# Seventh product behind the sixth and third in every Strassen group, and the decay rows spread in two parts

## The chip, the cores and the metric

The kernel runs on one core of one Trainium2 chip. The metric is the device time of one execution in microseconds. The kernel before was timed three times: 1894.62 us in the median, 1892.29 at the lowest and 1895.87 at the highest.

## The reference

Two blocks of a language model follow one another on 256 tokens of 2048 features, all in fp32. What matters here are the matrix products of the second block and the weights that they read:

```
merged = sigmoid(g_a) * (y_a @ w_up_a) + sigmoid(g_b) * (y_b @ w_up_b)   # g_a, g_b: columns of h @ w_in
x = x + merged @ w_o
hid = rmsnorm(x) @ w_ffn_in            # 2048 x (2 * 5632)
x = x + (silu(hid[:, :5632]) * hid[:, 5632:]) @ w_ffn_out
x = x + sigmoid(rmsnorm(x) @ w_ple_gate) * (p @ w_ple)
```

The first block has two recurrent layers ahead of its output product, an mLSTM with decay factors for each token and head, and an HGRN2 whose output h_b of 1024 features is normalised per head. Both lie beside the products of the first block's weights.

## The kernel before

**Pieces.** Every weight matrix is cut into pieces of two 128-row chunks by 512 columns (two such chunks, 512 KB in all). Piece g goes through four stations in a ring of four buffers (RING = 4). SyncE loads it into `raw`. ScalarE writes the high part of its fp32 values (`whi`, line 928, or line 1177 in a Strassen group), once TensorE has finished piece g-4. VectorE writes the rest (`wlo`, line 1876, or `s_lo`, line 2556). TensorE multiplies the high and low part of the activations by `whi` and the high part by `wlo`: twelve products of 128x512 for a standard piece (lines 1359 and 1364), six for a Strassen piece (lines 1724 and 1728). Every engine runs through the pieces in one written order, and whatever else an engine does is put between two pieces by a test on g or on (slab, piece).

**Strassen groups.** Twelve groups c = 0 to 11 compute two slabs of output columns by Strassen's seven products: groups 0 to 2 give the gates of the merge (`w_in`), groups 3 to 11 gates of the feed-forward part (`w_ffn_in`). A product M1 to M7 has four quarters q along the 2048 rows, so a group has 28 pieces in `S_ORDER`. `add_block` weaves them with standard pieces of other matrices: in most groups ten, one ahead of about every four Strassen pieces; the last group has 16. The products take their weights from different places:

- M1 from b11, loaded into the four quarters of `r1`; M5 from a sum that lies in the DRAM tensor `summed`, loaded into `r1` once M1's pieces are split (`load_fifth`, 1 MB twice).
- M2 from b21, M7 from another sum in `summed` ("seventh"): halves of 512 KB (`load_half`, line 788). M6's addend and M3's weights are both b22, also a half. All halves share the four slots raw[4..7]. `plan_s_loads` hands the slots out in the order of first use; a load waits until the piece that read its slot last has been split (`lo_ready`).
- M6 from r1 + b22, added by VectorE two Strassen pieces ahead (`s_sum`, line 2551, `S_LEAD` = 2).
- M4 from r1 + b21, added in place by an accumulating DMA of GpSimd (line 898), issued when M6.q has been split.

SyncE issues all its loads in one sorted order and waits at each until its place is free. `s_copies` (ScalarE) copies the sums of M1, M5 and M6 out of PSUM, `s_gates` (VectorE, three operations) forms the outputs after the last of M3 and M7, `s_silu` or sigmoids follow. M6 adds onto the sums of M1 and M3 onto those of M5, each once they have been copied; M7 has a PSUM bank of its own. `u_product` (VectorE) multiplies a product of `w_up_a` or `w_up_b` by its gate.

**Ahead of the groups.** `ml_cols` (TensorE) stands after piece (10, 7) of the first block: four transposes of 4x4, then eight products of 4x256 that spread rows of decay factors over 128 partitions into two PSUM buffers ("bc", 0) and ("bc", 1). VectorE reads them in slab 11. The scaling of hB, one half at a time (w counts VectorE's steps, L0 is 23 or 49), stands at step L0 + 30, line 2251; `hg_qd` and `hg_kd` (lines 2018 to 2027) are operands of TensorE's line 1431.

Of the kernel before, what the change touches and what calls it, by code (L numbers as in the profile page):

```python
# [39 lines left out]
S = 256  # L40
# [71 lines left out]
S_GROUPS = len(BLOCKS)  # L112
S_ORDER = [(m, q) for m in ("M1", "M2", "M7", "M5") for q in range(4)] \
    + [("M6", 0), ("M6", 1), ("M3", 0), ("M6", 2), ("M3", 1), ("M6", 3), ("M3", 2), ("M3", 3)] + [("M4", q) for q in range(4)]
S_LEAD = 2
# [199 lines left out]
def two_blocks_kernel(nc, A, out):  # L315
# [4 lines left out]
    with ctx:  # L320
# [338 lines left out]
        def _(sp):  # L659
# [130 lines left out]
            for free, need, kind, to, what in PLAN.loads:  # L790
                copies_for_sums(need)
                if kind == "pair":
                    load_ffn(free, need, to, what)
                if kind == "r1":
                    load_r1(free, to, what)
                if kind == "fifth":
                    load_fifth(free, to, what)
                if kind == "half":
                    load_half(free, to, *what)
                if kind == "resid":  # L800
                    sp.wait_ge(lo_ready, free + 1)
                    sp.wait_ge(piece_used, S_AT[M_GROUPS - 1, "M3", 3] + 1)
                    sp.wait_ge(sem("resid_held"), 16)
                    sp.dma_start(resid[:, :, to * COLS:(to + 1) * COLS], held[:, :, to * COLS:(to + 1) * COLS])\
                        .then_inc(sem(f"resid_back{to}"), 16)
                if kind == "p":
                    u_used(sp, "uB", 2)
                    sp.wait_ge(sem("p_held"), 32)
                    for x in range(2):
                        sp.dma_start(pT[1][x].bitcast(F32).rearrange("p k s -> p (k s)"), held_p[:, x]).then_inc(sem("p_back"), 16)  # L810
# [95 lines left out]
        def _(act):  # L906
# [272 lines left out]
            def s_copies(g, c):  # L1179

                if g == S_AT[c, "M2", 3]:
                    s_done(act, c, "M1")
                    if 0 < c < M_GROUPS and MERGE_S[c] == 2:
                        u_used(act, "uA", 0)
                    act.activation(hid_of(c)[:, 0, :], s_bank(c, "M1"), ACT.Copy).then_inc(sem("s_first"), 1)
                if g == S_AT[c, "M5", 3] + 3:
                    s_done(act, c, "M5")
                    if 0 < c < M_GROUPS:
                        u_used(act, "uB", max(0, MERGE_S[c] - 2))
                    act.activation(second_of(c)[:, 1, :], aux[:, 1, :], ACT.Copy).then_inc(sem("s_fifth"), 1)  # L1190
                if g == S_AT[c, "M6", 3] + 3:
                    act.wait_ge(piece_used, S_AT[c, "M6", 3] + 1)
                    act.activation(second_of(c)[:, 0, :], s_bank(c, "M6"), ACT.Copy).then_inc(sem("s_sixth"), 1)
# [6 lines left out]
            for kind, g, *x in PLAN.merge:  # L1200
# [22 lines left out]
                for c in range(M_GROUPS):  # L1223
                    s_copies(g, c)
                    if g == S_AT[c, "M3", 3] + 7:
                        act.wait_ge(sem("s_gate_in"), c + 1)
# [39 lines left out]
            for kind, g, *x in PLAN.ffn:  # L1266
# [22 lines left out]
                for c in range(M_GROUPS, S_GROUPS):  # L1289
                    s_copies(g, c)  # L1290
                    if g == S_AT[c, "M3", 3] + 7:
                        s_silu(c)


            for t, (g, n, role, _, q, p) in enumerate(PLAN.tail):
                split_hi(g)
                if g == S_AT[S_GROUPS - 1, "M3", 3] + 7:
                    s_silu(S_GROUPS - 1)
# [23 lines left out]
        def _(pe):  # L1322
# [161 lines left out]
            def ml_cols():  # L1484
# [7 lines left out]
                ins.then_inc(aux_full, 1)  # L1492
                for i in range(2):
                    u = AUX[("bc", i)]
                    free(u)
                    for h in range(2):
                        ins = pe.matmul(bank(u)[:, h * S:(h + 1) * S], sel[:, 2 * i + h, :], hrow[:, 3, :], start=True, stop=True)
                    ins.then_inc(aux_full, 1)

# [23 lines left out]
            for s in range(16):  # L1523
                n = FIRST["A"] + s
                for p in range(8):
# [25 lines left out]
                    if (s, p) == (10, 7):  # L1551
                        ml_cols()
                    if (s, p) == (11, 4):
                        ml_scores()
# [129 lines left out]
            def s_piece(g, c, m, q):  # L1684
# [12 lines left out]
                if m == "M2" and q == 0 and c > 0:  # L1697
                    pe.wait_ge(sem("hid_odd_ready"), c)
                    pe.wait_ge(sem("tr_taken"), fills_before(g, "a"))
                if m == "M7" and q == 0:  # L1700
                    pe.wait_ge(sem("merge_forms_lo" if c < M_GROUPS else "forms_lo"), 4)
# [162 lines left out]
        def _(dve):  # L1864
# [335 lines left out]
            for s in range(16):  # L2200
                for p in range(8):
# [22 lines left out]
                    for half, L0 in enumerate(HG_START):  # L2224
# [20 lines left out]
                        if w == L0 + 27:  # L2245
                            dve.wait_ge(sem("ss_hB"), half + 1)
                            variance(f"hB{half}", HG_E)
                        if w == L0 + 30:
                            powered(dve, f"hB{half}")
# [316 lines left out]
            def s_gates(c):  # L2566

                s_done(dve, c, "M3")
                dve.wait_ge(sem("s_sixth"), c + 1)
# [33 lines left out]
            for kind, g, *x in PLAN.merge:  # L2603
# [25 lines left out]
                for j in range(4):  # L2629
                    for role in ("uA", "uB"):  # L2630
                        if g == slab_end(role, j) + (2 if slab_end(role, j) in PLAN.block_end else 3):
                            u_product(role, j)
                for c in range(M_GROUPS):
                    if g == S_AT[c, "M2", 3] + 3:
                        s_up(c)
                    if g == S_AT[c, "M3", 3] + 3:
                        s_gates(c)
# [82 lines left out]
            def between(g):  # L2720
# [12 lines left out]
                for c in range(M_GROUPS, S_GROUPS):  # L2733
                    if g == S_AT[c, "M2", 3] + 3:
                        s_up(c)
                    if g == S_AT[c, "M3", 3] + 3:
                        s_gates(c)
# [113 lines left out]
```

## Time and profile before

| | |
|---|---|
| median of three runs | 1894.62 us |
| lowest, highest | 1892.29, 1895.87 us |
| profiled execution | 1893.05 us |
| its span | 1891.3 us |
| granted clock of TensorE, mean | 0.999 |

The page has for each engine its busy time and its share of the span:

| engine | busy us | share |
|---|---|---|
| TensorE, products | 1877.2 | 99% |
| TensorE, weight loads | 1641.9 | 87% |
| VectorE | 1471.8 | 78% |
| ScalarE | 1140.8 | 60% |
| GpSimd | 130.4 | 7% |
| DMA queue of SyncE, share of 16 engines | | 63.3% |
| DMA queue of GpSimd, share of 16 engines | | 20.6% |

A row of a timeline says when an instruction (or a run of equal ones) began, how long it ran, its line, what it wrote and read, and in brackets how long its engine had been idle before it and what released it. `ple<-...` in the groups is `r1`, which shares its memory. The chain of work that ended last consists of TensorE for 90%, VectorE for 5% and DMA for 3% of the span.

### The profile page before, as it was taken

How to read it: one execution, taken by the hardware profiler on the slowest of the kernel's cores; microseconds unless marked ns; L12 is line 12 of the kernel's file. 1: busy time of each engine (PE TensorE's matmuls, PEld its weight loads, DVE VectorE, ACT ScalarE, POOL GpSimd, SP SyncE). 2: the span in 40 equal slices, each digit the busy share in tenths (PEclk: the TensorE clock that was granted, in tenths of full speed). 3: DMA queues.
4: the chain of work that ended last, by engine and by line, in shares of the span. 5: the costliest groups of instructions: out<-in, count | busy, mean ns of one | idle time of the engine just before them, and what ended most of it. 6: DMA issues, size and time to landing. Idle time of an engine off the chain costs nothing.

```text
span 1891.3 us, 23371 instructions
## 1 busy us (share of the span) xinstructions
PE 1877.2 (99%) x9018; PEld 1641.9 (87%) x9018; DVE 1471.8 (78%) x1591; ACT 1140.8 (60%) x1417; POOL 130.4 (7%) x156
## 2 busy tenths in 40 slices
PE   9999999999999999999999999999999999999998
PEld 8888888888888888888888888888888888888887
DVE  6889776655666677778888657988998999898865
ACT  7556445555566556566766455666766676666553
POOL 4000011000001100000000000000000000000000
PEclk9999999999999999999999999999999999999999
DMA  9799898999989879998797886788878887987653
GB/s 392 267 284 310 274 309 272 330 347 327 309 290 312 271 269 299 321 315 278 295 313 247 330 256 239 254 311 284 276 254 320 280 271 257 327 260 249 219 188 130
DMA packets 86815, 535.95 MB, mean 283 GB/s; under 512 B 10416, under 2 KB 11184, under 8 KB 40752
## 3 DMA queue, kind: packets, MB, share of 16 engines
q1 hardware_dynamic: 72736, 458.69, 63.3%
q0 software_dynamic: 13824, 75.50, 20.6%
q8 instruction: 72, 1.18, 0.2%
q10 hardware_dynamic: 144, 0.26, 0.0%
q14 instruction: 39, 0.32, 0.0%
HBM read 529.69 MB, written 105.38 MB: 336 GB/s over the span
## 4 chain that ended last, share of the span: by engine, by line
PE 90%; DVE 5%; DMA 3%; issue 1%; ACT 1%; POOL 0%; SPq 0%; ACTq 0%; DVEq 0%; POOLq 0%
PE acc L1359 44%; PE acc L1364 22%; PE aux L1724 12%; PE aux L1728 6%; DVE wlo L2556 2%; PE aux L1338 2%; DMA ple<-in_w_ffn_in 1%; DVE wlo L1876 1%; PE aux L1431 1%; DVE ple L2551 1%; DMA ple<-in_w_in 1%; DMA raw<-summed 1%; PE aux L1805 0%; ACT whi L928 0%; ACT whi L1177 0%
## 5 line engine op out<-in xcount | busy, mean ns | idle before, releaser
L1876 DVE TENSOR_TENSOR wlo<-raw,whi 128x1024 fp32r<-128x1024 f32 x512 | 623.8, 1226 | 296.4 <-ACT whi L928 288.4
L928 ACT ACTIVATE whi<-raw 128x1024 fp32r<-128x1024 f32 x511 | 534.0, 1054 | 449.8 <-PE acc L1364 414.1
L1359 PE MATMUL acc<-whi,actA_hi 128*128 128x512 f32 x892 | 344.0, 386 | 0.7 <-ACT whi L928 0.7
L1359 PE MATMUL acc<-whi,actA_lo 128*128 128x512 f32 x892 | 339.1, 380 | 0.0
L1359 PE MATMUL acc<-whi,actB_hi 128*128 128x512 f32 x796 | 304.5, 383 | 0.2 <-DVE actB_lo L2673 0.2
L1359 PE MATMUL acc<-whi,actB_lo 128*128 128x512 f32 x796 | 301.7, 379 | 0.0
L1177 ACT ACTIVATE whi<-ple 128x1024 fp32r<-128x1024 f32 x192 | 201.0, 1055 | 139.4 <-PE acc L1364 55.6
L2556 DVE TENSOR_TENSOR wlo<-ple,whi 128x1024 fp32r<-128x1024 f32 x192 | 230.2, 1220 | 31.3 <-ACT whi L1177 28.5
L1364 PE MATMUL acc<-wlo,actA_hi 128*128 128x512 f32 x892 | 229.1, 379 | 0.0
L1364 PE MATMUL acc<-wlo,actB_hi 128*128 128x512 f32 x796 | 204.4, 379 | 0.0
L2556 DVE TENSOR_TENSOR wlo<-raw,whi 128x1024 fp32r<-128x1024 f32 x144 | 174.2, 1220 | 30.6 <-ACT whi L1177 28.9
L1359 PEld LDWEIGHTS acc<-whi,actA_hi 128*128 128x128 f32 x892 | 169.1, 190 | 25.5 <-issue 2.0
L1177 ACT ACTIVATE whi<-raw 128x1024 fp32r<-128x1024 f32 x144 | 152.0, 1055 | 64.3 <-PE acc L1364 36.5
L1364 PEld LDWEIGHTS acc<-wlo,actA_hi 128*128 128x128 f32 x892 | 168.9, 189 | 24.2
L1359 PEld LDWEIGHTS acc<-whi,actA_lo 128*128 128x128 f32 x892 | 169.2, 190 | 23.4 <-issue 0.5
L1359 PEld LDWEIGHTS acc<-whi,actB_hi 128*128 128x128 f32 x796 | 150.5, 189 | 21.6 <-DVE actB_lo L2673 1.0
L1364 PEld LDWEIGHTS acc<-wlo,actB_hi 128*128 128x128 f32 x796 | 150.4, 189 | 21.6 <-DVE wlo L1876 0.3
L1359 PEld LDWEIGHTS acc<-whi,actB_lo 128*128 128x128 f32 x796 | 150.6, 189 | 20.6
L1724 PE MATMUL aux<-whi,actB_hi 128*128 128x512 f32 x360 | 136.8, 380 | 0.8 <-ACT whi L1177 0.8
L1724 PE MATMUL aux<-whi,actB_lo 128*128 128x512 f32 x360 | 136.4, 379 | 0.0
L1728 PE MATMUL aux<-wlo,actB_hi 128*128 128x512 f32 x360 | 107.4, 380 | 0.9 <-DVE wlo L2556 0.8
L1724 PE MATMUL aux<-whi,actA_hi 128*128 128x512 f32 x216 | 83.0, 384 | 0.0
(366 smaller groups left out, 2377.0 us busy)
## 6 DMA issues: line engine op xcount, KB each, us to landing
raw<-in_w_in SPq DMA_DIRECT2D x108, 1024.0 KB, 7.3
raw<-in_w_ffn_out SPq DMA_DIRECT2D x44, 1024.0 KB, 6.9
summed<-in_w_ffn_in POOLq DMA_DIRECT2D x36, 1024.0 KB, 11.6
raw<-in_w_ffn_in SPq DMA_DIRECT2D x72, 512.0 KB, 7.9
ple<-summed SPq DMA_DIRECT2D x24, 1024.0 KB, 4.9
raw<-summed SPq DMA_DIRECT2D x48, 512.0 KB, 5.4
ple<-in_w_ffn_in SPq DMA_DIRECT2D x18, 1024.0 KB, 6.9
ple<-in_w_ffn_in POOLq DMA_DIRECT2D x36, 512.0 KB, 9.9
```

Of the source, the lines that this page charges most:

```text
L928: act.activation(whi[:, g % RING], raw_piece(g), ACT.Copy).then_inc(hi_ready, 1)
L1177: act.activation(whi[:, g % RING], s_source(c, m, q), ACT.Copy).then_inc(hi_ready, 1)
L1338: ins = pe.transpose(bank(u)[:, c * S + t * P:c * S + (t + 1) * P], src[:, t, (c0 + c) * P:(c0 + c + 1) * P], ident[:, :])
L1359: pe.matmul(acc2(n)[:, t, :], act[x][:, k + c, t * P:(t + 1) * P], woven(whi, g, c), start=(p == 0 and c == 0 and x == 0), stop=False)
L1364: ins = pe.matmul(acc2(n)[:, t, :], act[0][:, k + c, t * P:(t + 1) * P], woven(wlo, g, c), start=False, stop=(last and c == PK - 1))
L1431: ins = pe.matmul(bank(u)[:, c], Kp[n % 2][:, c], Qp[n % 2][:, c], start=True, stop=True)
L1724: pe.matmul(o, lhs(x, q * PK + k), woven(whi, g, k), start=(q == 0 and k == 0 and x == 0 and not onto), stop=False, skip_group_check=onto)
L1728: ins = pe.matmul(o, lhs(0, q * PK + k), woven(wlo, g, k), start=False, stop=(q == 3 and k == PK - 1), skip_group_check=onto)
L1876: dve.tensor_tensor(wlo[:, g % RING], raw_piece(g), whi[:, g % RING].bitcast(F32), ALU.subtract)\
L2551: dve.tensor_tensor(x, x, half_slot(c, S_ADDEND[m], q), ALU.add).then_inc(sem("s_sum"), 1)
L2556: dve.tensor_tensor(wlo[:, g % RING], s_source(c, m, q), whi[:, g % RING].bitcast(F32), ALU.subtract)\
```

## The change

In every group M7 moves from behind M2 to behind M6 and M3, and M6 and M3 take turns strictly: M1, M2, M5, then M6.0, M3.0, M6.1, M3.1, M6.2, M3.2, M6.3, M3.3, then M7, M4. What hung on the last piece of M3 (`s_gates`, `s_silu`, a load of `resid`) hangs on the last of M7; a wait for the summed activations moves from M7 to M5, the copy of M5 comes one piece earlier, and `u_product("uB", 2)` two pieces later. In the first block the eight spreading products are cut into four after piece (10, 7) and four after (11, 0), and the scaling of hB stands one step later.

```diff
-S_ORDER = [(m, q) for m in ("M1", "M2", "M7", "M5") for q in range(4)] \
-    + [("M6", 0), ("M6", 1), ("M3", 0), ("M6", 2), ("M3", 1), ("M6", 3), ("M3", 2), ("M3", 3)] + [("M4", q) for q in range(4)]
+S_ORDER = [(m, q) for m in ("M1", "M2", "M5") for q in range(4)] \
+    + [(m, q) for q in range(4) for m in ("M6", "M3")] + [(m, q) for m in ("M7", "M4") for q in range(4)]
...
-                    sp.wait_ge(piece_used, S_AT[M_GROUPS - 1, "M3", 3] + 1)
+                    sp.wait_ge(piece_used, S_AT[M_GROUPS - 1, "M7", 3] + 1)
...
-                if g == S_AT[c, "M5", 3] + 3:
+                if g == S_AT[c, "M5", 3] + 2:
...
-                    if g == S_AT[c, "M3", 3] + 7:
+                    if g == S_AT[c, "M7", 3] + 7:
...
-                for i in range(2):
-                    u = AUX[("bc", i)]
-                    free(u)
-                    for h in range(2):
-                        ins = pe.matmul(bank(u)[:, h * S:(h + 1) * S], sel[:, 2 * i + h, :], hrow[:, 3, :], start=True, stop=True)
-                    ins.then_inc(aux_full, 1)
+
+            def ml_rows_spread(i):
+                u = AUX[("bc", i)]
+                free(u)
+                for h in range(2):
+                    ins = pe.matmul(bank(u)[:, h * S:(h + 1) * S], sel[:, 2 * i + h, :], hrow[:, 3, :], start=True, stop=True)
+                ins.then_inc(aux_full, 1)
...
                         ml_cols()
+                        ml_rows_spread(0)
+                    if (s, p) == (11, 0):
+                        ml_rows_spread(1)
...
-                if m == "M7" and q == 0:
+                if m == "M5" and q == 0:
                     pe.wait_ge(sem("merge_forms_lo" if c < M_GROUPS else "forms_lo"), 4)
...
-                        if w == L0 + 30:
+                        if w == L0 + 31:
...
-                s_done(dve, c, "M3")
+                s_done(dve, c, "M7")
...
-                        if g == slab_end(role, j) + (2 if slab_end(role, j) in PLAN.block_end else 3):
+                        last = slab_end(role, j)
+                        if g == last + (2 if last in PLAN.block_end else 5 if (role, j) == ("uB", 2) else 3):
...
-                    if g == S_AT[c, "M3", 3] + 3:
+                    if g == S_AT[c, "M7", 3] + 3:
                         s_gates(c)
```

## Rows read from the trace of the kernel before

**Rows 1.** The page's head and its first part.

```profile
span 1891.3 us, 23371 instructions
...
PE 1877.2 (99%) x9018; PEld 1641.9 (87%) x9018; DVE 1471.8 (78%) x1591; ACT 1140.8 (60%) x1417; POOL 130.4 (7%) x156
```

**Rows 2.** Waits of the weight load, 840 to 1800 us: us in total, times, longest us.

```profile
PEld aux L1728 <- DVE wlo L2556: 4.7, 8, 1.2
PEld aux L1724 <- ACT whi L1177: 1.8, 3, 1.2
```

**Rows 3.** Timeline of TensorE around 1028: start us, us, line, xcount [idle before <-releaser].

```profile
1025.47 0.38 PE L1724 MATMUL aux<-whi,actB_hi 128*128 128x512 f32 x1
...
1026.76 0.38 PE L1724 MATMUL aux<-whi,actB_hi 128*128 128x512 f32 x1
...
1028.58 0.70 PE L1728 MATMUL aux<-wlo,actB_hi 128*128 128x512 f32 x2 [0.79 <-DVE wlo L2556]
1029.12 0.38 PE L1359 MATMUL acc<-whi,actA_hi 128*128 128x512 f32 x1
```

**Rows 4.** Timeline of ScalarE at 863 and at 1025.

```profile
863.26 1.06 ACT L1177 ACTIVATE whi<-raw 128x1024 fp32r<-128x1024 f32 x1 [4.64 <-DMA raw<-summed]
...
1025.02 1.06 ACT L1177 ACTIVATE whi<-ple 128x1024 fp32r<-128x1024 f32 x1 [3.41 <-DMA ple<-in_w_in]
```

**Rows 5.** Timeline of TensorE, 273.8 to 280.5.

```profile
274.14 1.97 PE L1497 MATMUL aux<-hrow,sel 4*128 4x256 f32 x8
276.04 0.51 PE L1359 MATMUL acc<-whi,actA_hi 128*128 128x512 f32 x1
...
280.42 0.38 PE L1359 MATMUL acc<-whi,actA_hi 128*128 128x512 f32 x1
```

**Rows 6.** Stretches: from:to length, busy (xcount) per engine, PEclk, DMA share, GB/s.

```profile
276.30:279.80 3.50, 3.50 (x10) 2.72 (x10) 3.46 (x11) 0.00 (x0) 0.00 (x0) 0.51 1.04 274
218.00:219.70 1.70, 0.00 (x0) 0.00 (x0) 1.66 (x4) 0.00 (x0) 0.00 (x0) 1.00 1.05 188
```

**Rows 7.** Timeline of VectorE, 156 to 162.

```profile
158.79 1.22 DVE L2251 TENSOR_TENSOR hg_v<-hg_v,rstd 128x1024 f32<-128x1024 f32 x1
```

**Rows 8.** Timeline of TensorE, 160 to 162.7.

```profile
161.46 1.16 PE L1431 MATMUL aux<-hg_qd,hg_kd 128*128 128x128 f32 x8 [0.75 <-DVE hg_kd L2027]
```

**Rows 9.** Timeline of ScalarE, 1206 to 1212.

```profile
1206.90 1.06 ACT L1177 ACTIVATE whi<-ple 128x1024 fp32r<-128x1024 f32 x1 [0.24 <-PE aux L1728]
```

**Rows 10.** Timeline of VectorE, 1204 to 1212.

```profile
1206.70 3.82 DVE L2556 TENSOR_TENSOR wlo<-ple,whi 128x1024 fp32r<-128x1024 f32 x3
1210.43 1.22 DVE L2551 TENSOR_TENSOR ple<-ple,raw 128x1024 f32<-128x1024 f32 x1
```

**Rows 11.** Timeline of GpSimd's DMA issues, 1279 to 1300.

```profile
1280.96 0.86 POOL L898 DMA_DIRECT2D ple<-in_w_ffn_in  x1 [54.12 <-DVE wlo L2556]
1282.09 0.86 POOL L898 DMA_DIRECT2D ple<-in_w_ffn_in  x1 [0.27 <-DVE wlo L2556]
1287.05 0.86 POOL L898 DMA_DIRECT2D ple<-in_w_ffn_in  x1 [4.10 <-DVE wlo L2556]
1291.59 0.86 POOL L898 DMA_DIRECT2D ple<-in_w_ffn_in  x1 [3.68 <-DVE wlo L2556]
```

**Rows 12.** Timeline of SyncE's DMA issues, 1276 to 1300.

```profile
1279.56 0.33 SPq L763 DMA_DIRECT2D raw<-in_w_ffn_out  x1
1284.10 9.83 SPq L788 DMA_DIRECT2D raw<-in_w_ffn_in  x4
```

**Rows 13.** DMA, 1280 to 1300: queues, then issues (KB each, median us to landing).

```profile
q0 software_dynamic: 576, 2.10, 56.2%
q1 hardware_dynamic: 653, 2.94, 40.6%
...
ple<-in_w_ffn_in POOLq DMA_DIRECT2D x4, 512.0 KB, 8.9
raw<-in_w_ffn_in SPq DMA_DIRECT2D x4, 512.0 KB, 8.5
```

**Rows 14.** DMA, 1343 to 1360: issues.

```profile
raw<-in_w_ffn_in SPq DMA_DIRECT2D x4, 512.0 KB, 9.8
```

**Rows 15.** The page's sixth part: DMA issues.

```profile
raw<-summed SPq DMA_DIRECT2D x48, 512.0 KB, 5.4
```

**Rows 16.** Groups of instructions by line, VectorE.

```profile
L2718 DVE TENSOR_TENSOR resid<-resid,acc 128x1024 f32<-128x1024 f32 x20 | 24.3, 1213 | 0.4 <-PE acc L1364 0.4
```

More of the change, by code:

```diff
@@ L1290, in _ @@
                     s_copies(g, c)
-                    if g == S_AT[c, "M3", 3] + 7:
+                    if g == S_AT[c, "M7", 3] + 7:
                         s_silu(c)
@@ L1296, in _ @@
                 split_hi(g)
-                if g == S_AT[S_GROUPS - 1, "M3", 3] + 7:
+                if g == S_AT[S_GROUPS - 1, "M7", 3] + 7:
                     s_silu(S_GROUPS - 1)
@@ L2735, in between @@
                         s_up(c)
-                    if g == S_AT[c, "M3", 3] + 3:
+                    if g == S_AT[c, "M7", 3] + 3:
                         s_gates(c)
```

## Prediction, made before the change was run

> **What bounds the kernel now.** I read the page's head first: TensorE is busy 1877.2 of 1891.3 us [rows 1], and its mean granted clock is 0.999 of full speed, so the time is the number of its columns plus its gaps. The profiled run took 1893.05 us with 1.75 us outside its span; the median of the three timed runs, 1894.62 us, is 1.57 us more, and I add that at the end. The change adds and removes no product of any size. It can therefore only close gaps, open gaps, or change the clock. The next views are the waits ahead of TensorE over the Strassen groups [rows 2], one gap of each kind in the timelines [rows 3 to 8], and then what the new order leans on: how far ScalarE and VectorE run ahead [rows 9, 10] and what the DMA queues do while M6 and M3 run [rows 11 to 15].
>
> Six products of a Strassen piece take 1.29 us from start to start (1025.47 to 1026.76) [rows 3], so a standard piece of twelve takes 2.59. I count time from the start of M5.0 in the new order. The places are M5.0 to M5.3 at 0, 1.3, 2.6, 3.9; a standard piece at 5.2; M6.0 7.8, M3.0 9.1, M6.1 10.4, M3.1 11.7; standard 13.0; M6.2 15.5, M3.2 16.8, M6.3 18.1, M3.3 19.4; standard 20.7; M7.0 to M7.3 at 23.3, 24.6, 25.9, 27.2; standard 28.5; M4.0 at 31.1.
>
> **What it takes away.**
> (a) The waits for M4. M4's weights are r1 plus b21, added by a POOL DMA that starts when M6.q is split. In the group at 1028 M4.3 starts 1.29 after M4.2, but its last products wait for the low half of its weights, and the next piece starts at 1029.12: 2.36 for a piece of 1.29, a gap of 1.06 [rows 3]. ScalarE began that split at 1025.02 after 3.41 us of waiting for the DMA [rows 4]; at VectorE it then stood in the queue. Over the groups the eight waits for the low half add up to 4.7 us [rows 2]. M6.3 moves four pieces towards the front (three Strassen, one standard: 3 x 1.29 + 2.59 = 6.5 us), more than 3.41, so these waits go. u_product(uB,2) moves behind one more piece and has no consumer near: nothing.
> (b) M7's weights in the first group come by loads that end too late: ScalarE waits at 863.26 for 4.64 us [rows 4], TensorE 1.8 us in three waits [rows 2]. M5 takes that place; its two loads are issued as soon as M1's pairs of quarters are split, ahead of M7's in the same queue, and a wait of TensorE for them shows nowhere. So these go. (a) and (b) are 6.5 us by the waits; each wait also costs some 0.1 to 0.2 of restart that the row doesn't count, so I take 7.0.
> (c) The spread of the decay rows. Eight four-row products take 1.97 us [rows 5]; right behind them the granted clock is 0.51 of full speed, its 1.2 GHz level, for 3.5 us [rows 6], and the piece from 276.04 to 280.42 takes 4.38 instead of 2.59 [rows 5]: 1.8 us. With four of them behind (10,7) and four behind (11,0), 1 us each, a full piece stands between. An idle engine over 1.7 us left the clock at 1.00 [rows 6], so a lone 1 us of small products ought not to lower it. I take 1.8 us as gained; the other bound is nothing gained. The second part is read by vector work three pieces later: no wait.
> (d) The scaling of the first half of hB, 1.22 us of VectorE at 158.79 [rows 7], stands ahead of the products of the gate that TensorE waits for 0.75 us at 161.46 [rows 8]. One step later it stands behind them, and the gap shrinks from 0.75 plus restart to nothing: 1.0 us. For the second half there is no such wait on the page: nothing.
> Together 7.0 + 1.8 + 1.0 = 9.8 us.
>
> **What it adds: a wait for M7's weights.** M7's four halves ("seventh", 512 KB each, from `summed`) share four slots with b21 and b22, given out in order of first use. In the old order M7 came before M6 and took the slots that M2 had freed. Now M7 comes after M3, and each of its loads waits until M3.q has been split. So when is M3.q split? ScalarE starts the split of piece g 0.24 us after TensorE has left piece g-4 and takes 1.06 [rows 9]; VectorE takes 1.22 for the low half, 3.82 for three, and 1.22 more for each sum of M6.q [rows 10]. Through nine splits and four sums VectorE is the later of the two. Stepping through the places gives the ends of the M3 splits at 8.2, 11.6, 16.2 and 18.4. Counting back from the products that read the low half (0.86 into a piece), a split must start 1.44 us ahead of its piece: at 21.9, 23.2, 24.4 and 25.7 for M7.0 to M7.3. The four loads thus have 13.7, 11.6, 8.2 and 7.3 us.
>
> How long do they take? In the old order the same moment had the same traffic, with b21 of the next group in M7's place: four adds from 1280.96 to 1291.59 [rows 11], a 1 MB load at 1279.56 and four halves from 1284.10 [rows 12]. There the halves took 8.5 us in the median, the adds 8.9 [rows 13]; in another group 9.8 [rows 14]. Alone, a load from `summed` takes 5.4 [rows 15], but the adds are now all under way beside M7's loads (issued 5.4 to 17.6). By single loads M7.3 lands at 18.4 + 8.5 = 26.9 or 18.4 + 9.8 = 28.2, against 25.7: 1.2 or 2.5 us late. By volume: the software queue took 56.2% of 20 us for 2.10 MB, four adds, so 2.8 us of all sixteen engines each; the hardware queue 40.6% for 2.94 MB, so 1.45 for a half and 2.9 for 1 MB [rows 13]. Four adds, four halves and the 1 MB load are 19.9 us. From the first issue at 5.4, with some 2.5 us in which little moves (the start of the first transfer, and the thin start of the queue), all is landed at 27.8: 2.1 late. I take 2.0 us of stall for M7.3, with 1.2 and 2.5 as ends. M7.2 (16.2 + 8.5 = 24.7 against 24.4) stalls by part of it only.
>
> The groups 0 to 10 are alike; the last one has 16 standard pieces between, over 10 us from M3.3 to M7.3, and no stall. 11 x 2.0 = 22 us. After such a stall VectorE has no lead, and in three groups an addition to the residual (1.21 us) [rows 16] falls on M4: 0.8 each, 2.4 us. Elsewhere the extra vector operations keep at least 0.5 us of slack. The gates, their activations and the load of `resid` hang on M7.3 now instead of M3.3; each is the last piece ahead of M4 and the standard piece before it, so nothing there moves. M5's copy on ScalarE comes a piece earlier and finds 2 us of slack; the loads of M5 and of M6's addends are issued no later than before and are needed 15 us on: nothing.
>
> **Sum.** 22 + 2.4 - 9.8 = +14.6 us: 1893.05 + 14.6 = 1907.7, and with the 1.57 of the median 1909.2. I forecast 1909.
>
> The Trainium skill speaks against this price. Its page "DMA: Bandwidth & Descriptors", section "Anatomy of one DMA — SWDGE (gpsimd) path", gives about 2 us plus the bytes over 436 GB/s; an estimate by it is 3.2 us for 512 KB, below the 7.3 allowed, and the sum would be -9.8. The 8.5 to 9.8 us of these rows disagree wherever adds run beside the load. The same page's "Arbitration" says that a DMA engine turns between its queues packet by packet, which agrees with those rows.
>
> **Rivals.**
> (B) M7's loads are in time. If they take 7.3 us or less, no stall: 1893.05 - 9.8 = 1883.3, median 1884.8. For it: the 5.4 us of a load alone [rows 15], and the M3 splits are spread over 10 us, so that the adds are thinner than at 1280. Against it: all groups' medians that I read lie at 8.5 or above in that stretch, and the volume leaves no room.
> (C) A small stall. At 0.9 us per group, 10 us, the gains are used up: 1894.6. It wants halves of 8.2 us.
> (D) Heavier. With 9.8 us for each, M7.2 is 1.6 late and M7.3 2.5; 11 x 2.5 = 27.5, + 3.5 behind it, - 9.8 = +21: 1916. If such a gap lowers the clock for 3.5 us as at 276, 1.8 us more in each hit group; for half of them +10: 1926.
> (E) The split of the small products doesn't hold the clock up: +1.8 on any case. A part of each range, not a case of its own.
>
> **How the numbers follow.** A difference within 0.2% (3.8 us) can't be told from none. Forecast (stalls of 1.2 to 2.5; 1899 to 1916): 0.66. D: 0.13. C, which ends within 0.2%: 0.11. B, faster: 0.10. Of the forecast's lowest part little falls under 1898.4, so slower is 0.78, same 0.12, faster 0.10. The range leaves out B and the end of D: 1892 to 1924.
>
> **What would show it.** In the changed kernel: ScalarE's L1177 waiting for `raw<-summed` ahead of M7.3, and TensorE gaps of some 2 us at L1724 or L1728 in M7 eleven times; the seventh halves at 8 to 10 us instead of 5.4; no gap at M4.3; M5 at 864 without one; the granted clock at 1.00 from 276 to 280; no wait at L1431 near 161. Wrong it is if the halves issued behind the M3 splits take under 7.3 us, or if those splits end well before 18.4.

## The result, and the profile after

The changed kernel takes 1936.64 us in the median of four runs (1931.02 to 1938.94), against 1893.68 for the kernel before (median of four, 1892.29 to 1895.87): a ratio of 1.022, 95% interval 1.0202 to 1.0239. The forecast was 1909, with a range up to 1924. The direction was right and the size was not: +43 us instead of +14.6.

The page of the changed kernel, its head, its first part, one group of the fifth and three of the sixth (issues: KB each, median us to landing):

```profile
span 1935.5 us, 23369 instructions
...
PE 1892.7 (98%) x9018; PEld 1649.4 (85%) x9018; DVE 1471.0 (76%) x1591; ACT 1138.9 (59%) x1417; POOL 130.7 (7%) x156
...
L1177 ACT ACTIVATE whi<-raw 128x1024 fp32r<-128x1024 f32 x144 | 151.7, 1054 | 108.3 <-DMA raw<-summed 78.0
...
raw<-in_w_ffn_in SPq DMA_DIRECT2D x72, 512.0 KB, 5.0
...
raw<-summed SPq DMA_DIRECT2D x48, 512.0 KB, 8.2
...
ple<-in_w_ffn_in POOLq DMA_DIRECT2D x36, 512.0 KB, 9.0
```

No engine has more to do than before; TensorE's share fell from 99% to 98% and its busy time rose from 1877.2 [rows 1] to 1892.7, which is the sign of a lower clock, since the products are the same 9018: the mean granted clock fell from 0.999 to 0.992. The halves from `summed` take 8.2 us in the median instead of 5.4 [rows 15], and ScalarE spends 78.0 us waiting for them.

The waits of the weight load from 840 to 1900 us, which answer to [rows 2]:

```profile
PEld aux L1728 <- ACT whi L1177: 35.6, 14, 4.1
PEld aux L1732 <- DVE wlo L2560: 6.7, 11, 1.0
```

Before, these two rows were 1.8 us in three waits and 4.7 in eight. Now the high part of a piece is waited for in 14 places, 35.6 us.

One group of the eleven begins with M5.0 at 1279.64. SyncE's issues in the timeline of the changed kernel, which answer to [rows 12]:

```profile
1287.85 3.73 SPq L788 DMA_DIRECT2D raw<-summed  x2
1292.39 0.33 SPq L763 DMA_DIRECT2D raw<-in_w_ffn_out  x1
1295.80 4.23 SPq L788 DMA_DIRECT2D raw<-summed  x2
```

GpSimd's issues in the same timeline, which answer to [rows 11]:

```profile
1285.14 0.86 POOL L898 DMA_DIRECT2D ple<-in_w_ffn_in  x1 [55.12 <-DVE wlo L2560]
1289.25 0.86 POOL L898 DMA_DIRECT2D ple<-in_w_ffn_in  x1 [3.25 <-DVE wlo L2560]
1293.79 0.86 POOL L898 DMA_DIRECT2D ple<-in_w_ffn_in  x1 [3.68 <-DVE wlo L2560]
1297.29 0.86 POOL L898 DMA_DIRECT2D ple<-in_w_ffn_in  x1 [2.63 <-DVE wlo L2560]
```

ScalarE at M7.2 and M7.3 in that timeline:

```profile
1307.08 1.06 ACT L1177 ACTIVATE whi<-raw 128x1024 fp32r<-128x1024 f32 x1 [6.27 <-DMA raw<-summed]
1308.36 1.06 ACT L1177 ACTIVATE whi<-raw 128x1024 fp32r<-128x1024 f32 x1 [0.22 <-DMA raw<-summed]
```

TensorE from M7.1's last products to the standard piece behind M7.3, which answers to [rows 3]:

```profile
1305.11 0.59 PE L1732 MATMUL aux<-wlo,actB_hi 128*128 128x512 f32 x2
1308.19 0.48 PE L1728 MATMUL aux<-whi,actB_hi 128*128 128x512 f32 x1 [2.48 <-ACT whi L1177]
...
1309.45 1.22 PE L1732 MATMUL aux<-wlo,actB_hi 128*128 128x512 f32 x2
1310.46 0.63 PE L1728 MATMUL aux<-whi,actB_hi 128*128 128x512 f32 x1
...
1312.69 0.38 PE L1359 MATMUL acc<-whi,hidT_x_hi 128*128 128x512 f32 x1
```

The chain of waits of the changed kernel through the same stretch (start us, us, what):

```profile
1295.80 11.26 DMA raw<-summed
...
1307.08 1.06 ACT whi L1177
...
1308.19 1.37 PE aux L1728 x4
```

The 2.9 us behind the gap in its view by stretches, with the columns of [rows 6]:

```profile
1308.10:1311.00 2.90, 2.81 (x8) 1.96 (x9) 2.78 (x3) 2.68 (x4) 0.00 (x0) 0.64 0.76 287
```

M7.2's load was issued at 1295.80 and took 11.26 us. The gap ahead of M7.2 is 2.48 us, the one before its low part 0.3 more, and then M7.2's last products and all of M7.3's start 0.43 us apart instead of 0.216: M7.3, at 1310.46, is over at 1312.69 after 2.23 us instead of 1.29. The granted clock is 0.64 of full speed on average over these 2.9 us, a mixture of both levels.

The edits outside the groups. TensorE's timeline of the changed kernel at the two parts of the spread, which answers to [rows 5]:

```profile
275.75 1.10 PE L1498 MATMUL aux<-hrow,sel 4*128 4x256 f32 x4
...
279.57 1.12 PE L1498 MATMUL aux<-hrow,sel 4*128 4x256 f32 x4
```

The stretch around them, and the one behind the long wait at 219, in its view by stretches:

```profile
275.75:280.70 4.95, 4.95 (x24) 3.56 (x22) 3.94 (x8) 1.91 (x2) 0.00 (x0) 1.00 1.04 286
220.00:223.00 3.00, 3.00 (x16) 3.00 (x16) 2.89 (x7) 0.00 (x0) 0.00 (x0) 0.51 1.01 175
```

The clock is full around the spread (0.51 behind it before [rows 6]). It is 0.51 from 220 to 223, where it was 1.00 before. TensorE at L1431, which answers to [rows 8], and at the wait for `ml_qk`:

```profile
160.91 1.05 PE L1431 MATMUL aux<-hg_qd,hg_kd 128*128 128x128 f32 x8
...
219.80 0.56 PE L1452 MATMUL aux<-hg_v,hg_a 128*128 128x128 f32 x2 [2.62 <-DVE ml_qk L2079]
```

The waits of the weight load at L1431 from 100 to 230 us:

```profile
PEld aux L1431 <- DVE hg_kd L2031: 1.2, 4, 0.4
```

### The profile page after: what moved, and what is told of

The parts are those of the page before. It is cut to its first block, busy times and chain, and to the rows that moved or that the text cites. A ratio compares the mean times of both kernels' runs of the same rounds, so it can differ in the third digit from the quotient of the medians.

```text
span 1935.5 us, 23369 instructions
## 1 busy us (share of the span) xinstructions
PE 1892.7 (98%) x9018; PEld 1649.4 (85%) x9018; DVE 1471.0 (76%) x1591; ACT 1138.9 (59%) x1417; POOL 130.7 (7%) x156
## 4 chain that ended last, share of the span: by engine, by line
PE 76%; DVE 11%; DMA 8%; ACT 2%; issue 2%; POOL 0%; SPq 0%; ACTq 0%; DVEq 0%; POOLq 0%
PE acc L1359 39%; PE acc L1364 19%; PE aux L1728 8%; DMA raw<-summed 6%; DVE wlo L2560 6%; PE aux L1732 4%; DVE ple L2555 2%; DVE wlo L1880 2%; PE aux L1338 2%; DMA raw<-in_w_in 1%; ACT whi L1177 1%; PE aux L1431 1%; DMA ple<-summed 1%; ACT whi L928 1%; PE aux L1809 0%
## 5 line engine op out<-in xcount | busy, mean ns | idle before, releaser
L1177 ACT ACTIVATE whi<-raw 128x1024 fp32r<-128x1024 f32 x144 | 151.7, 1054 | 108.3 <-DMA raw<-summed 78.0
L1364 PEld LDWEIGHTS acc<-wlo,actA_hi 128*128 128x128 f32 x892 | 168.6, 189 | 23.9
L1728 PE MATMUL aux<-whi,actB_hi 128*128 128x512 f32 x360 | 141.5, 393 | 21.4 <-ACT whi L1177 21.4
L1732 PE MATMUL aux<-wlo,actB_hi 128*128 128x512 f32 x360 | 111.1, 391 | 0.8
L1728 PEld LDWEIGHTS aux<-whi,actB_hi 128*128 128x128 f32 x360 | 70.1, 195 | 35.6 <-ACT whi L1177 25.4
## 6 DMA issues: line engine op xcount, KB each, us to landing
summed<-in_w_ffn_in POOLq DMA_DIRECT2D x36, 1024.0 KB, 11.6
```

The source lines that it names most:

```text
L1177: act.activation(whi[:, g % RING], s_source(c, m, q), ACT.Copy).then_inc(hi_ready, 1)
L1364: ins = pe.matmul(acc2(n)[:, t, :], act[0][:, k + c, t * P:(t + 1) * P], woven(wlo, g, c), start=False, stop=(last and c == PK - 1))
L1728: pe.matmul(o, lhs(x, q * PK + k), woven(whi, g, k), start=(q == 0 and k == 0 and x == 0 and not onto), stop=False, skip_group_check=onto)
L1732: ins = pe.matmul(o, lhs(0, q * PK + k), woven(wlo, g, k), start=False, stop=(q == 3 and k == PK - 1), skip_group_check=onto)
```

## The experiments

All start times that follow are us behind the start of M5.0 in the group, as in the prediction, and medians over the groups 0 to 10. M7.2's load must have landed at 24.4, M7.3's at 25.7 for no gap.

**The two edits outside the groups alone.**

```diff
# the kernel before, with
+                        ml_rows_spread(0)
...
+                    if (s, p) == (11, 0):
+                        ml_rows_spread(1)
...
-                        if w == L0 + 30:
+                        if w == L0 + 31:
```

> The kernel before with only the two edits outside the groups: the eight spreading products cut into four and four, and hB scaled one step later. The prediction's sum says -1.8 and -1.0: 1890.9 in the median, no half clock at 276 to 280, no wait of L1431 near 161. Reading of the changed kernel's trace: the spread gives 1.3, and the later scaling gives nothing, since its 0.6 us are gone again at 210, where TensorE waits for VectorE in any case (the wait for ml_qk stands at 219.8 in both traces); and whether the clock falls behind that wait is a matter of chance (1.4 us). That gives 1891 to 1895, which can hardly be told from before; the trace between 120 and 225 us decides.

Measured: 1892.52 us against 1893.92, ratio 0.9994 (0.9984 to 1.0003): no difference that can be told. In the trace the stretch from slab 10.5 to slab 12.0 is 1.3 us shorter and no product of it runs at half clock. The stretch that holds the gate of HGRN2 (pieces 40 to 60) is 0.55 us shorter and pieces 60 to 72 are 1.8 us longer. Of these 1.6 stand behind the wait for `ml_qk`, where the clock was at half, as in the changed kernel; the rest are small waits at L1431. The half clock is not the edit's doing, as the kernel with M6 earlier (below) shows: it has neither edit and runs at half clock in the same place. Its view by stretches:

```profile
220.00:223.00 3.00, 2.28 (x11) 2.28 (x12) 2.89 (x7) 0.00 (x0) 0.00 (x0) 0.64 1.01 210
```

The same view of the kernel before has 1.00 in this stretch; the wait itself is 2.62 us there, 2.61 and 2.62 in the others. So the same gap is followed by full clock in one execution and by half clock in another: full in two of the twelve profiled executions (the kernel before and the one with the last two adds alone), half in ten.

**No adds.** M4 then reads r1 without b21; this part of the computation is left out.

```diff
-                                pool.dma_start(r1[:, q], s_weights(c, what, q), accum_op=ALU.add).then_inc(sem(f"r1_added{q}"), 16)
+                                pool.sem_inc(sem(f"r1_added{q}"), 16)
```

> The changed kernel without the accumulating DMAs of GpSimd, so M4 reads r1 without b21 added (this part of the computation is left out). Theory A (M7's halves are late because they share the DMA engines with the adds and stand in one queue behind a 1 MB load): the halves issued at 16.2 and 18.4 us behind M5.0 take under 7 us instead of 11.7 and 10.8, the gaps ahead of M7.2 and M7.3 go in all of the eleven groups, the clock falls in none, and the time is that of before less the gains in the groups: 1884 to 1889. Theory B (reads from `summed` are slow in themselves, or VectorE is late in the strict turn of M6 and M3): the gaps stay at 3 to 5 us per group, 1925 to 1937.

Measured: 1886.09 us (1885.80 to 1886.57), ratio 0.9959 (0.9945 to 0.9974). M7.2's load takes 4.8 us instead of 11.7 and M7.3's 4.0 instead of 10.6; they land at 21.2 and 22.8. From 840 us to the end of the run one row of waits remains, for the activations of the last stage:

```profile
PEld acc L1359 <- DVE actB_lo L2678: 1.0, 2, 0.6
```

So `summed` is no slow source and VectorE is not late. Theory A holds as far as the adds are a necessary part of it. Of the 7.8 us below the kernel before, 7.2 are won in the groups (pieces 290 to 762 of the trace), where the prediction had said 7.0.

**One quarter of M7 ahead of M6.**

```diff
+S_ORDER = [(m, q) for m in ("M1", "M2", "M5") for q in range(4)] + [("M7", 0)] \
+    + [(m, q) for q in range(4) for m in ("M6", "M3")] + [("M7", 1), ("M7", 2), ("M7", 3)] + [("M4", q) for q in range(4)]
```

> The changed kernel with M7.0 between M5 and M6.0; M7.1 to M7.3 stay behind M3.3. The slots then go round one further: M7.1 to M7.3 wait for the split of M3.0 to M3.2, some 9.5, 14.5 and 17.5 us behind M5.0 instead of 11.6, 16.2 and 18.4, and one half less is in the way. Theory A: M7.2, 3.7 us late in the changed kernel, comes 0 to 1.5 late; no half clock behind most of the gaps: 1888 to 1903. Theory B (what matters is the order of M6 and M3, or the source): M7.2 and M7.3 stay 3 us late, 1925 or more.

Measured: 1938.42 us, ratio 1.0236 (1.0221 to 1.0252), as slow as the changed kernel. Theory A's number is missed by 35 us. Theory B names the time, but the kernel without adds has ruled out its reasons, the source and a late VectorE. In the trace the loads wait for one M3 less, but that M3 itself stands a piece later, so that M7.2's is issued only 1 us earlier, at 15.1. It still stands behind the 1 MB load, and the adds are later as well: it takes 12.1 us and lands at 27.2, M7.3's takes 11.5 and lands at 30.0 (in the group at 1281, one of the best, 10.55 us and 25.6 for M7.2). The waits of the weight load from 840 us:

```profile
PEld aux L1728 <- ACT whi L1177: 35.6, 19, 5.1
PEld aux L1732 <- DVE wlo L2560: 16.5, 26, 1.2
```

Of the 16.5 us of L1732, 2.7 (from start to start) stand at M6.3 in four groups, where the changed kernel has none; why VectorE is late there was not taken apart. An issue 1 us earlier didn't help a load that stands in such a queue.

**All adds behind M3.3.**

```diff
-                                pool.wait_ge(lo_ready, S_AT[c, before, q] + 1)
+                                pool.wait_ge(lo_ready, S_AT[c, "M3", 3] + 1)
```

> The changed kernel with all four adds of a group issued only when M3.3 has been split (18.4 us behind M5.0), behind M7's last load; nothing is left out. Theory A: M7's halves take about 5 to 6 us and are in time; the adds are 11.2 us of all engines and land at about 22, 26, 29 and 32 against 29.6 to 33.5 at which M4 needs them: no gap, or one of up to 1 us at M4.3: 1886 to 1898, at or below the time of before. Theory B: as the changed kernel, 1930 and more.

Measured: 1975.73 us, ratio 1.0438 (1.0420 to 1.0455). Half of theory A came true: M7's loads take 3.4 to 4.1 us in the group at 1295, and in M7 one gap is left, of 0.7 us in the third group. But the adds come far too late: the weight load waits for the high part in 31 places, 63.0 us, nearly all in M4. GpSimd issues the four together, by its timeline:

```profile
1315.13 3.54 POOL L898 DMA_DIRECT2D ple<-in_w_ffn_in  x4 [68.71 <-DVE wlo L2560]
```

and ScalarE's timeline shows when it gets the weights of M4.0 to M4.3:

```profile
1323.26 1.06 ACT L1177 ACTIVATE whi<-ple 128x1024 fp32r<-128x1024 f32 x1 [2.54 <-DMA ple<-in_w_ffn_in]
1327.08 1.06 ACT L1177 ACTIVATE whi<-ple 128x1024 fp32r<-128x1024 f32 x1 [2.75 <-DMA ple<-in_w_ffn_in]
1330.89 1.06 ACT L1177 ACTIVATE whi<-ple 128x1024 fp32r<-128x1024 f32 x1 [2.76 <-DMA ple<-in_w_ffn_in]
1334.72 1.06 ACT L1177 ACTIVATE whi<-ple 128x1024 fp32r<-128x1024 f32 x1 [2.77 <-DMA ple<-in_w_ffn_in]
```

One add lands every 3.82 us, not every 2.8. The loads issued beside them (the next group's halves of b21) land at 1327.22, 1331.05 and 1334.87 by their issue records, each within 0.2 us of an add. So while adds are queued SyncE's queue lands one load of 512 KB per add. I took from this a price per 512 KB, so that a load of 1 MB would need two adds; this replaces the volume of the prediction as theory C of the next runs. The step to 1 MB was wrong, as the changed kernel's own trace shows. Its 1 MB load lands 5.0 us behind M7.1's (3.7 to 5.3 over the groups), not 7.6, and M7.2's half 3.8 us behind that.

The packets tell why. A transfer is moved in packets, and a view lists for each queue the packets, the MB and the share of the 16 engines. Between the first and the second landing of the late adds, 1323.3 to 1327.0:

```profile
q0 software_dynamic: 137, 0.50, 67.1%
q1 hardware_dynamic: 138, 0.50, 35.9%
```

In the changed kernel, 1298.4 to 1300.2, while the 1 MB load is moved beside an add:

```profile
q0 software_dynamic: 46, 0.19, 52.2%
q1 hardware_dynamic: 43, 0.35, 48.8%
```

Both queues get about the same number of packets, so a load goes forward packet for packet with an add. A packet of the 1 MB load carries 8 KB (0.35 MB in 43) and one of a half or an add 4 KB, so either load lasts as many packets as one add; those of 8 KB only take longer.

**The 1 MB load behind M7's loads.**

```diff
+        for c in range(S_GROUPS - 1):
+            a, b = self.s_at[c, "M6", 0], self.s_at[c, "M3", 3]
+            self.loads = [(b, *x[1:]) if x[2] == "pair" and a <= x[0] < b else x for x in self.loads]
         self.loads.sort(key=lambda x: (x[0], x[1]))
```

> The changed kernel with one 1 MB load per group moved: the pair of standard pieces that SyncE issues 12.8 us behind M5.0, ahead of M7.2's and M7.3's loads, is issued behind M7.3's (its pieces are needed 36 us behind M5.0). Nothing is left out. Theory C (loads of SyncE land strictly one behind the other, and while an add is under way the queue lands only 512 KB in about 3.8 us, as the four adds issued together in the previous runs showed, against 1.25 us without adds): 1 MB less in the queue brings M7.2's landing from 27.4 to some 22.4, ahead of the 24.4 it is needed at, and M7.3's to 24 to 26 against 25.7: gaps of 0 to 0.5 us per group, 1885 to 1894. Theory D (each transfer shares evenly with all others in flight, so one fewer of four only shortens it by a fourth): M7.2 lands 1 to 2 us late still, 1905 to 1920.

Measured: 1902.99 us, ratio 1.0043 (1.0030 to 1.0056). M7.2's load takes 6.8 us instead of 11.7 and lands at 23.3, in time (theory C said 22.4). M7.3's is issued at 19.0, takes 8.2 and lands at 26.9, 1.2 late; theory C said 24 to 26, and the measured time is 9 us above its upper end. Theory D's 1905 to 1920 is missed as well, from the other side. The waits that are left:

```profile
PEld aux L1731 <- ACT whi L1180: 10.3, 12, 1.5
PEld aux L1735 <- DVE wlo L2563: 9.3, 15, 1.0
```

M7.2's landing moves by 4.6 us, which fits the 5.0 that the 1 MB load took beside an add. One load of 1 MB in another place of the queue is worth 34 of the 43 us.

**The adds of M4.2 and M4.3 alone, and those of M4.0 and M4.1 alone.** The other two are left out of the computation each time. The second kernel has `q >= 2` in the place of `q < 2`.

```diff
-                                pool.dma_start(r1[:, q], s_weights(c, what, q), accum_op=ALU.add).then_inc(sem(f"r1_added{q}"), 16)
+                                if q < 2:
+                                    pool.sem_inc(sem(f"r1_added{q}"), 16)
+                                else:
+                                    pool.dma_start(r1[:, q], s_weights(c, what, q), accum_op=ALU.add).then_inc(sem(f"r1_added{q}"), 16)
```

> The changed kernel with the adds of M4.2 and M4.3 alone (those of M4.0 and M4.1, issued 5.4 and 9.7 us behind M5.0, are left out of the computation). Theory C: the queue is empty when the 1 MB load is issued at 12.8, but from 14.2 on an add is always under way, so 1 MB and M7.2's half take some 2 to 3 turns of 3.8 us: M7.2 lands at 22 to 24, no gap or one under 1 us; M7.3 at 24 to 26: 1886 to 1900. If the backlog of all four adds is not what counts, but the adds beside M7.2's load alone, M7.2 still takes 10 us or more and the gaps stay near 3 us: 1915 to 1935.

> The changed kernel with the adds of M4.0 and M4.1 alone (those of M4.2 and M4.3 are left out). Theory C: after about 17 us behind M5.0 no add is under way, and M7.2's and M7.3's halves take 4 to 5 us: no gap, 1884 to 1888. If it is the backlog of the first two adds that makes M7 late: gaps of 1 us and more, above 1895.

Measured, one run each: 1913.35 us with the last two adds, 1886.56 with the first two. With the last two, M7.2's load takes 8.6 us and lands at 24.8, M7.3's 9.0 and 28.1. Theory C's landings and its 1886 to 1900 are missed, and so is the other branch (10 us or more for M7.2, 1915 to 1935), though by less. With the first two, they take 6.2 and 4.9, land at 22.4 and 23.9, and no gap is left, as without any add. It is the two adds issued at 14.2 and 17.6 that hold M7's loads up; the first two cost no gap alone, but add their backlog to these (24.8 becomes 27.9 with all four).

**The old order with M6.2 and M6.3 one place earlier.**

```diff
-    + [("M6", 0), ("M6", 1), ("M3", 0), ("M6", 2), ("M3", 1), ("M6", 3), ("M3", 2), ("M3", 3)]
+    + [("M6", 0), ("M6", 1), ("M6", 2), ("M3", 0), ("M6", 3), ("M3", 1), ("M3", 2), ("M3", 3)]
```

> The kernel before with M6.2 and M6.3 one place earlier each (M6.0, M6.1, M6.2, M3.0, M6.3, M3.1, M3.2, M3.3), M7 ahead of M5 as before; nothing else is changed. The adds of M4.2 and M4.3 start 1.3 to 2.6 us earlier. If the waits at M4.3 (some 5 us in all) come from the late start of the add, half or more of them go: 1889 to 1893. If VectorE, which has one sum more early, or the halves of b22 become late: gaps of about 1 us in M6, 1895 to 1905.

Measured: 1894.73 against 1894.24, ratio 1.0001 (0.9992 to 1.0010). Both things happen: from start to start the gaps at M4.3 shrink (0.9 us left ahead of its low part), and VectorE, which has a sum more to make, is late at M3.0 in five groups by 2.5 us. Nothing is won. The waits of the weight load for low parts, 6.0 us in nine places against 4.7 in eight [rows 2]:

```profile
PEld aux L1728 <- DVE wlo L2556: 6.0, 9, 1.1
```

**The last add later as well.** The 1 MB load stays behind M7's loads, and the add of M4.3 waits for M7.0's split.

```diff
-                                pool.wait_ge(lo_ready, S_AT[c, before, q] + 1)
+                                pool.wait_ge(lo_ready, (S_AT[c, "M7", 0] if q == 3 else S_AT[c, before, q]) + 1)
```

> The kernel of e5 (the 1 MB load behind M7.3's) with one more shift: the add of M4.3 is issued once M7.0 has been split, some 20.9 us behind M5.0 instead of 17.6; nothing is left out. If the landings of SyncE's queue are held back by the adds one for one, M7.3's half (20.1 at the latest to issue) has only the end of the add of M4.2 beside it and lands at 24 to 25, in time for 25.7; the add of M4.3 takes 8 to 10 us and lands at 29 to 31 against 33.5. Then no gap is left in the groups and the time is that of the kernel without adds, 1886 to 1890, below before. If the loads wait for something else than the adds (the 1 MB loads of the standard pieces behind them), M7.3 stays 1 us late and M4.3 may come late as well: 1898 to 1908.

Measured: 1887.08 us (1885.83 to 1887.36), ratio 0.9962 (0.9948 to 0.9975): faster than the kernel before by 7.4 us (0.4%, a small difference, but the interval leaves out 1) and than the changed one by some 50, with the whole computation. M7.2's load lands at 23.0, M7.3's takes 4.9 us instead of 8.2 and lands at 24.3. The add of M4.3, issued at 1283.46, lets ScalarE begin at 1293.28, and no gap follows. ScalarE's timeline at M7.2, M7.3 and M4.3:

```profile
1284.11 1.06 ACT L1180 ACTIVATE whi<-raw 128x1024 fp32r<-128x1024 f32 x1 [2.08 <-DMA raw<-summed]
1285.71 1.06 ACT L1180 ACTIVATE whi<-raw 128x1024 fp32r<-128x1024 f32 x1 [0.55 <-DMA raw<-summed]
...
1293.28 1.06 ACT L1180 ACTIVATE whi<-ple 128x1024 fp32r<-128x1024 f32 x1 [2.61 <-DMA ple<-in_w_ffn_in]
```

The only row of waits of the weight load behind 840 us is the one for the last stage's activations:

```profile
PEld acc L1362 <- DVE actB_lo L2681: 1.0, 2, 0.6
```

**That later add alone, the 1 MB load where the change put it.**

```diff
# the changed kernel, with
-                                pool.wait_ge(lo_ready, S_AT[c, before, q] + 1)
+                                pool.wait_ge(lo_ready, (S_AT[c, "M7", 0] if q == 3 else S_AT[c, before, q]) + 1)
```

> The changed kernel with the later add of M4.3 alone (the 1 MB load stays ahead of M7.2's half); nothing is left out. With the queue in order, M7.2's half still stands behind 1 MB that lands at 23.6 beside the add of M4.2; then it takes 1.3 to 3 us more: 25 to 26.5 against 24.4, M7.3 just behind. Gaps of 1 to 2.5 us per group: 1900 to 1915, between the changed kernel and e5. If the order in the queue doesn't matter, M7.2 is in time, 1890 or less.

Measured, one run: 1912.72 us. M7.2's load lands at 25.2 (25 to 26.5 said), M7.3's at 27.5; the waits are 17.8 us for the high part and 12.8 for the low one. The order in the queue matters. The later add alone is worth 24 us and the 1 MB load alone 34, both together 50.

The kernels with the new order, without the one with all adds late, whose loads for M7 are in time (21.3 and 23.8) and whose time is lost in M4 (medians of the groups 0 to 10, landing behind M5.0, needed at 24.4 and 25.7):

| kernel | M7.2: took, landed | M7.3: took, landed | median us |
|---|---|---|---|
| changed | 11.7, 27.9 | 10.6, 29.2 | 1936.6 |
| last two adds | 8.6, 24.8 | 9.0, 28.1 | 1913.4 |
| last add later | 8.8, 25.2 | 8.8, 27.5 | 1912.7 |
| 1 MB later | 6.8, 23.3 | 8.2, 26.9 | 1903.0 |
| 1 MB and last add later | 6.8, 23.0 | 4.9, 24.3 | 1887.1 |
| first two adds | 6.2, 22.4 | 4.9, 23.9 | 1886.6 |
| no adds | 4.8, 21.2 | 4.0, 22.8 | 1886.1 |

The time follows the landings, M7.3's too where M7.2's is in time.

## Why the prediction was wrong in size

**The slot and the issue times were right.** The halves of M7 were issued at 8.2, 11.6, 16.2 and 19.0; the prediction said 8.2, 11.6, 16.2 and 18.4, so only the last was 0.6 early. The deadlines of 24.4 and 25.7 fit too: the kernels without a gap in M7 have landings of 23.0 and 24.3 at the latest, and the one with 24.8 and 28.1 waits.

**The step that failed is the time of M7.2's load.** The prediction took 8.5 us from the old order [rows 13], called the traffic the same, and let M7.2 be late by 0.3 us and M7.3 by 2.0. M7.2's took 11.7 and landed at 27.9, 3.5 us late. Two things were not the same as in the old order. The first is the moment of the 1 MB load. It was issued at 1279.56 [rows 12], ahead of the first add at 1280.96 [rows 11], and was through by 1285, with 26 packets of adds beside its own 144; in the new order the first two adds go ahead of it, and the M7.2 half stands behind it in the queue. Its rows, before and after, in the groups at 1275 and at 1280:

```profile
raw<-in_w_ffn_out SPq DMA_DIRECT2D x1, 1024.0 KB, 5.4
```

```profile
raw<-in_w_ffn_out SPq DMA_DIRECT2D x1, 1024.0 KB, 10.9
```

The second is what each load in the queue costs beside adds: 5.0 us for the 1 MB load and 3.8 for a half, not 2.9 and 1.45, since packets of the adds come in between. The volume sum of 19.9 us gave 27.8 for the last landing, 1.4 below the 29.2 measured. So even this sum would have told more had it been asked for M7.2: with 1.45 us less it is 26.4, 2 us past 24.4. The prediction asked it for the last load only, and took a single duration for the one before it.

**The clock was put into the rival with 0.13.** In seven of the eleven groups products behind the gap start 0.43 us apart. Counted over the trace from start to start, the groups lose 51.3 us, and pieces 290 to 762 take as much more than with the first two adds alone: 30.0 ahead of M7.2, 2.3 ahead of M7.3 (three groups), 2.6 ahead of their low parts (nine places), 1.5 at M4.3 (two groups), 12.0 in products at half clock and 3.0 in the restarts. The forecast had 22 + 2.4 for all of this. The waits alone, 36.3 us, would have stayed within the range, 1894.6 + 36.3 - 9.8 = 1921.1. The half clock, which the forecast put at nothing, took the time out of it.

**The gains in the groups were right.** 7.0 us predicted for the waits at M4 and in the first group's M7. Without a gap in M7 (first two adds alone) pieces 290 to 762 take 7.2 us less than before.

**The spread was right in kind, 0.5 us too high.** 1.3 instead of 1.8: the piece is at full clock, but the second part costs its own way in and out of the stream. The reason given for it was weak. The 1.00 of [rows 6] from 218.0 to 219.7 was read inside the wait for `ml_qk`, and behind that wait the clock was at half in ten of twelve executions.

**The scaling of hB was worth 0.4 us, not 1.0.** The wait at 161 went, and piece 52 starts 1.0 us earlier, as said. But smaller waits of the same line came: L1431 waited 1.1 us in one place before and 1.2 in four after, and 0.6 us were given back by piece 64. The rest was kept: from the start of piece 36 to the end of the wait for `ml_qk` it is 108.8 us in the two kernels without this edit and 108.3 to 108.4 in the ten with it. The end of that wait at 219.84 before and 219.80 after hides this, because the changed kernel's execution was 0.4 us behind at piece 36; that the gain is gone at 210, as was expected for the run of the two edits alone, did not come true.

**Rivals.** B was 1884.8 for loads in time; the kernels without gaps measure 1.3 to 2.3 us more, but its condition (7.3 us or less) was missed by over 3. D, with both M7.2 and M7.3 late and the lower clock, was the right mechanism, and still short: its 1926 counted gaps of 2.5 and the clock in half of the groups.

The Trainium skill's page "DMA: Bandwidth & Descriptors", section "Queues, rings and completion order" under "Arbitration", says that each DMA engine turns between its queues packet by packet. The trace agrees: 137 packets of the adds against 138 of the loads, and 46 against 43.

The prediction's estimate of 3.2 us rests on the Trainium skill's same page, section "Anatomy of one DMA — SWDGE (gpsimd) path". Its figure is for DMAs that GpSimd issues, and M7's loads are SyncE's. Without adds they took 3.6 to 4.8 us here (medians of the four halves), beside adds up to 12.1.

## What to carry over

Where a load moves behind a new event, look at what stands ahead of it in its own queue and what runs in the other queues, at the new moment; a median of the same size of load from the old order is no price for it. Ask the sum for each load that has a deadline, not for the last one alone, since the first late piece stops the engine. And the order in a queue can be changed: here moving one 1 MB load, needed some 9 us later than the loads behind it, and one add caused no wait elsewhere and was worth 50 us.

## What the runs showed of the hardware

- Beside accumulating DMAs of GpSimd, SyncE's queue lands one load of 512 KB per add, in step with it: 3.82 us for the pair, where the page's and the window's shares gave 2.8 + 1.45 = 4.25 us of the engines' time for both and 1.45 for the load alone. Without adds such loads land 1.2 to 1.3 us apart, as at 1307.06 to 1310.79 of the changed kernel, behind the last add.
- The two queues move packet for packet: 137 of the adds and 138 of the loads from 1323.3 to 1327.0 of the kernel with late adds, 46 and 43 from 1298.4 to 1300.2 of the changed one. The 1 MB loads have packets of 8 KB and the adds of 4 KB, so that beside adds a 1 MB load costs 5.0 us, and a half 3.8.
- The same 2.6 us wait of TensorE at 219 was followed by full clock in the profiled execution of the kernel before and by half clock in those of the changed kernel (0.51 over 3 us), of the ends alone and of the kernel with M6 earlier (0.64 over the same 3 us, which hold the end of the wait). Half clock followed in ten of the twelve profiled executions and cost 1.5 to 1.7 us from piece 69 to 72. Whether a gap costs clock is not told by its length in one trace. In the changed kernel the gaps of 0.9, 1.0, 1.5 and, once, 3.2 us ahead of M7.2 cost no product at half clock, and the other seven, of 2.6 to 3.8 us, did.
